# Up projection of a float32 encoder layer: both sequences together at each k tile instead of one after the other

## The reference

```python
up = _dwconv3(_rmsnorm(x, norm2) @ w_up, conv_w, conv_b)
gate, val = up[..., :D_FF], up[..., D_FF:]
x = x + (jax.nn.silu(gate) * val) @ w_down
```

## Time and profile before

| What | Value |
|---|---|
| median of 3 runs | 1347.67 us |
| span of the profiled execution, first to last instruction | 1343.5 us |
| TensorE busy | 1277.8 us, 95% of the span |
| VectorE busy | 820.0 us, 61% |
| ScalarE busy | 443.2 us, 33% |
| mean granted TensorE clock | 0.984 of full speed |
| matmuls and weight loads | 5487 each |

### The profile page before, as it was taken

One profiled execution on the slowest core, in us unless ns is written; L12 is line 12 of the kernel. 1 busy time (PEld: TensorE's weight loads), 2 busy tenths in 40 slices (PEclk: granted clock), 3 DMA queues, 4 the chain that ended last, 5 costly groups with the idle time before them and its releaser, 6 DMA issues.

```text
span 1343.5 us, 15745 instructions
## 1 busy us (share of the span) xinstructions
PE 1277.8 (95%) x5487; PEld 980.3 (73%) x5487; DVE 820.0 (61%) x1234; ACT 443.2 (33%) x711; POOL 175.3 (13%) x139
## 2 busy tenths in 40 slices
PE   6899699999999999999999999999999999979996
PEld 4687455555488778888888888888888888767885
DVE  5547786786456666565656565656565656594564
ACT  4311464564412352222222222222223231363233
POOL 0137400000065301010101010000000000060000
PEclk9999799999999999999999999999999999989999
DMA  5420000010343221111111111111111111012432
GB/s 177 174 55 10 10 11 0 10 31 1 110 141 94 95 79 47 48 47 47 47 47 47 47 47 47 47 47 47 47 47 47 47 47 47 8 32 82 130 112 91
DMA packets 103258, 78.76 MB, mean 59 GB/s; under 512 B 4707, under 2 KB 97210, under 8 KB 102458
## 3 DMA queue, kind: packets, MB, share of 16 engines
q1 hardware_dynamic: 102928, 78.23, 18.5%
q10 hardware_dynamic: 298, 0.11, 0.0%
HBM read 69.94 MB, written 8.39 MB: 58 GB/s over the span
## 4 chain that ended last, share of the span: by engine, by line
PE 79%; DVE 8%; issue 1%; ACT 1%; DVEq 0%; ACTq 0%
PE ps L184 24%; PE ps L186 24%; PE ps L185 24%; PE ps L491 3%; PE ps L479 2%; DVE XL L1372 1%; DVE XT L1208 1%; DVE SF L1185 1%; DVE XT L1188 1%; DVE XT L1184 1%; DVE XT L1333 1%; DVE col L1201 0%; DVE WDHL L1194 0%; DVE TL L1422 0%; PE ps L378 0%
## 5 line engine op out<-in xcount | busy, mean ns | idle before, releaser
L184 PE MATMUL ps<-XH,WH 128*128 128x512 f32 x1096 | 441.8, 403 | 5.3 <-DVE SF L1100 3.7
L185 PE MATMUL ps<-XL,WH 128*128 128x512 f32 x1096 | 436.5, 398 | 0.0
L186 PE MATMUL ps<-XH,WL 128*128 128x512 f32 x1096 | 436.3, 398 | 0.0
L184 PEld LDWEIGHTS ps<-XH,WH 128*128 128x128 f32 x1096 | 207.9, 190 | 59.1 <-DVE WL L197 6.5
L185 PEld LDWEIGHTS ps<-XL,WH 128*128 128x128 f32 x1096 | 207.8, 190 | 51.1 <-issue 1.9
L186 PEld LDWEIGHTS ps<-XH,WL 128*128 128x128 f32 x1096 | 207.7, 189 | 50.6
L1303 DVE TENSOR_TENSOR SF<-ps,R 128x512 f32<-128x512 f32 x88 | 60.6, 690 | 178.9 <-PE ps L186 173.4
L943 ACT ACTIVATE SF<-SF,col 128x512 f32<-128x512 f32 x88 | 71.8, 817 | 268.0 <-DVE SF L1303 268.0
L197 DVE TENSOR_TENSOR WL<-WR,WH 128x1024 fp32r<-128x1024 f32 (+2 forms) x93 | 119.8, 1293 | 61.9 <-ACT WH L192 61.9
L1333 DVE TENSOR_TENSOR XT<-XT,ps 128x512 f32<-128x512 f32 x176 | 116.7, 685 | 63.0 <-PE ps L186 63.0
L192 ACT ACTIVATE WH<-WR 128x1024 fp32r<-128x1024 f32 (+2 forms) x93 | 93.1, 1002 | 187.7 <-PE ps L186 179.0
(11 more groups left out here) (153 smaller groups left out, 1361.7 us busy)
## 6 DMA issues: line engine op xcount, KB each, us to landing
WR<-in_w_up SPq DMA_DIRECT2D x44, 512.0 KB, 3.8
SF<-in_w_down SPq DMA_DIRECT2D x11, 1024.0 KB, 4.9
WR<-in_w_out SPq DMA_DIRECT2D x16, 512.0 KB, 3.8
WR<-in_w_ple_gate SPq DMA_DIRECT2D x16, 512.0 KB, 3.9
WR<-in_w_in SPq DMA_DIRECT2D x8, 512.0 KB, 3.9
xt_scratch<-XT SPq DMA_DIRECT2D x2, 2048.0 KB, 13.0
XT<-xt_scratch SPq DMA_DIRECT2D x4, 1024.0 KB, 7.8
out<-TL SPq DMA_DIRECT2D x8, 512.0 KB, 2.7
```

What stands on the lines that cost most here:

```text
L184: pe.matmul(out, wh, xh, start=first, stop=False)
L185: pe.matmul(out, wh, xl, start=False, stop=False)
L186: return pe.matmul(out, wl, xh, start=False, stop=last)
```

## The change

A new function `up_both(i, c)` replaces `up(i, c)` for all up tiles but the first two of pair 0, which is 42 of 44. At each k tile it issues, for sequence 0 and then 1, high weights times the high and the low activation half; then low weights times the high half for both sequences. Both banks fill at the same time. The number of matmuls, their shapes and operands are the same. It waits once, for the banks of both sequences, ahead of its first matmul. `up_ready` is signalled by the last two matmuls.

```diff
+            def up_both(i, c):
+
+                n = T_UP + c
+                pe.wait_ge(w_lo, i * 4 + (n + 1))
+                if c >= 2:
+                    pe.wait_ge(u_ready, i * 8 + 2 * (c - 1))
+                else:
+                    pe.wait_ge(u_ready, i * 8 + (2 * c - 2))
+                for k in range(KT):
+                    wh, wl = WH[:, slot(n), k, :], WL[:, slot(n), k, :]
+                    for s in range(NSEQ):
+                        b = ps[2 * (c % 2) + s][:, :]
+                        pe.matmul(b, wh, XH[:, s, k, :], start=k == 0, stop=False)
+                        pe.matmul(b, wh, XL[:, s, k, :], start=False, stop=False)
+                    for s in range(NSEQ):
+                        b = ps[2 * (c % 2) + s][:, :]
+                        ins = pe.matmul(b, wl, XH[:, s, k, :], start=False, stop=k == KT - 1)
+                        if k == KT - 1:
+                            ins.then_inc(up_ready, 1)
+
...
-            up(0, 2)
-            up(0, 3)
+            up_both(0, 2)
+            up_both(0, 3)
             with pe.Fori(0, NPAIR // 2) as j:
                 for i in (j * 2 + 1, j * 2 + 2):
-                    up(i, 0)
-                    up(i, 1)
+                    up_both(i, 0)
+                    up_both(i, 1)
                     down(i - 1, 0)
                     down(i - 1, 1)
-                    up(i, 2)
-                    up(i, 3)
+                    up_both(i, 2)
+                    up_both(i, 3)
```

## The result

The changed kernel takes 1354.39 us (median of 5 runs, 1352.93 to 1355.83), the kernel before 1347.66 us (median of 5, 1344.03 to 1348.14). The ratio is 1.0049 with a 95% interval of 1.0036 to 1.0061: slower by 4.9 to 8.2 us.

A forecast was written before the change was run, and what follows sets the result against it. TensorE was taken as the bound, busy for all 512.80 us of the loop window, with no cover left at down tile 6. 1347.67 + 4.5 (ten holes) + 0.45 (last down) = 1352.6 us, range 1349.0 to 1357.0.

The forecast's parts named there:

- Step between matmuls: Up tiles: each matmul keeps its own weight load and the 234 ns step, bank switches costing 0.
- The faster rival: Up tiles: matmuls that repeat their weights come cheaper, 14.1 us saved less 4.95, giving 1338.5 us; chance 6%.
- the slower ones: Up tiles: alternating banks adds 12.1 us, 1364.7 us, chance 5%; or the clock falls to 1.2 GHz, adding 383 us, 1%.
- Delay of the adds: VectorE behind up tile 1: both `scaled` come behind the tile's end, so down's adds begin 0.45 us late.
- The pattern of pair 0: Pair 0 runs two `scaled` back to back, next work 4.27 us behind the first: lower bound of delay, 0.39 us.
- the loop's own ScalarE latency: In the loop ScalarE's middle tap begins 0.81 us behind the start of `scaled`: upper bound of delay, 0.49 us.
- One hole per pair, at down tile 6: TensorE stands 0.45 us at down tile 6, waiting for the third add, in 10 pairs: 4.5 us.
- Tile 4 with its 0.2 us of cover: Down tile 4: the delayed first add is done at 795.87, its weight load starts at 796.10, so just hidden.
- The last down: Outside the loop, TensorE's 4.61 us wait for the split of the gated result ends 0.45 us later.
- The sum: Whole kernel: +4.5 and +0.45 make +4.95 us on the median 1347.67, giving 1352.6 us.
- time outside the first and last instruction: Whole kernel: the median of the runs was taken as 4.2 us above the profiled span of 1343.5 us.
- The clock at the end: Behind the last down's wait: stretches at 1.2 GHz shift with the program, given ±1.6 us with mean 0.

The follow-up runs named there:

- the third add first: Changed kernel, and separately the kernel before, with VectorE's add of down tile 2 moved ahead of the next low-weight split: 1347.48 us and 1347.43 us.
- the first experiment: Changed kernel with up tile 1 inside the loop back to one sequence after the other, tiles 0, 2 and 3 still interleaved: 1348.82 us, ratio 1.0001.
- the second: Changed kernel with only up tile 1 of pairs 1 to 10 interleaved, all other up tiles in the old order: 1353.36 us, ratio 1.0036.

## Why the prediction was right, point by point

**Step between matmuls.** I took 234 ns for both orders. Right: up tile 1 takes 11.24 us in both, a pair with all up tiles interleaved takes 66.79 us where it takes 66.79 in the old order (both with the third add first), and the equality of loads and matmuls held. The faster rival (held weights pay) and the slower ones (banks, the clock) are out. The Trainium skill says in "TensorE: Matmul & The Clock Gate", section "Step-by-step: what each phase is for", that weights typically stay put over many matmuls, so that one load can serve them; this program issued a load for each, and nothing was gained. The same page of the Trainium skill tells, under "A second HAM failure mode: psum-queue depth-cycling", of a kernel whose clock swung while it cycled through banks; that did not come here, where the granted clock in the loop was 1.00 with the banks alternated.

**Delay of the adds.** Taken 0.45 us, bounds 0.39 and 0.49; measured 0.47. The pattern of pair 0 gave the lower bound, the loop's own ScalarE latency the upper one, and the truth lay nearer to the loop's.

**One hole per pair, at down tile 6.** Right in place and count, 0.48 us against 0.45; the wait of the weight load is 0.65 to 0.70 us where I wrote about 0.6. Tile 4 with its 0.2 us of cover did not wait.

**The last down.** +0.45 predicted, 5.08 - 4.61 = +0.47 measured. That it does not come from up tile 1 is shown by the first experiment, where it stays, and by the second, where it is gone. That of the other tiles it is up tile 3, the one directly ahead, was not tested by itself.

**The sum.** +4.95 predicted; 10 x 0.48 + 0.47 = 5.3 us by the trace. The runs give +6.7 us, interval 4.9 to 8.2, so the trace's 5.3 lies in it. The forecast of 1352.6 us is 1.8 us below the measured 1354.39, and 1.4 us of this is more than the mechanism explains. A part may be the median of before, which rests on five runs: the larger groups of runs beside the experiments give 1348.50 and 1348.22 us for the same kernel, 5.9 and 6.2 us below 1354.39.

One figure of the base was wrong: "time outside the first and last instruction" was taken as 4.2 us. In the profile after, the profiled execution itself took 1354.68 us with a span of 1352.8, so 1.9 us lie outside, and the runs of the kernel before that give both show about 2 (1344.03 and 1342.0). The profiled execution of before was then probably a short one of about 1345.4 us. The sum was made as a difference to the median, and so the mistake fell out of it. That also explains why the two spans differ by 9.3 us and the medians by 6.7.

**The clock at the end.** ±1.6 us. The profiled execution after had 0.74 of full clock in the 20 us in which the last down ends and the gate stage begins, and before had 0.83:

```profile
1208.90:1228.90 20.00, 13.96 (x53) 11.03 (x52) 11.65 (x17) 6.86 (x12) 7.75 (x6) 0.74 0.14 40
```

```profile
1200.20:1220.20 20.00, 13.98 (x56) 11.08 (x55) 12.07 (x18) 7.49 (x13) 7.75 (x6) 0.83 0.14 41
```

From the start behind the last down's wait to the end of the span it is 167.15 us after (1352.85 - 1185.70) and 166.49 before (1343.50 - 1177.01), 0.66 us more, well inside the ±1.6. Over all nine profiled executions (before, after, seven experiments) the three with 0.74 in this stretch take 167.15 to 167.46 us and the six with 0.83 take 166.27 to 166.61. So the clock here is worth about 1 us from one execution to the next. It is not tied to the longer wait: the kernel with only tile 1 interleaved has 0.74 with the wait of before. Whether it shifts the median of the changed kernel one profile can't say. What I had left out is the same effect ahead of the loop; the last section has it.

## What to carry to other kernels

Look first at where a consumer waits with no cover left, and count an edit by what it does to the last signal in front of that place; TensorE's order within the 11 us of an up tile changed nothing else here. A wait of 0.2 us in a list of waits can mean that the cover is just used up: here it cost 0.05 us per pair, and every delay beyond it counted in full, once in each pair: adds 0.47 us late cost 0.48 us, and adds 0.71 us late cost 0.72. A cure can be to move one instruction that is needed now ahead of one whose result is needed some 25 us later.

## What the runs showed of the hardware

The first down of the loop starts between 523.51 and 527.54 us in the nine profiled executions. The four up tiles ahead of it, the first that the change touches, account for none of this: they take 45.08 us in all nine, in the old order and the new. In the kernel before and in the changed one they begin at

```profile
478.43 0.50 PE L184 MATMUL ps<-XH,WH 128*128 128x512 f32 x1 [1.64 <-DVE WL L197]
```

```profile
481.88 0.50 PE L600 MATMUL ps<-XH,WH 128*128 128x512 f32 x1 [1.63 <-DVE WL L197]
```

and up to there all nine kernels do the same. The mean granted clock up to 523.5 us is 0.98 in the kernel before and 0.97 in the changed one:

```profile
0.00:523.50 523.50, 479.32 (x2027) 334.92 (x2028) 339.93 (x556) 213.48 (x390) 113.43 (x103) 0.98 0.21 66
```

```profile
0.00:523.50 523.50, 479.85 (x2013) 335.00 (x2014) 339.30 (x555) 212.05 (x389) 113.32 (x103) 0.97 0.20 65
```

The difference lies in the first 366 us; from there to 523.5 us the granted clock is 1.00 in all nine. Up to 366 us it is 0.97 in the two executions whose down starts first (523.51 and 524.08), 0.96 in two others (525.08 and 526.96) and 0.95 in the remaining five (525.32 to 527.54). The start goes with the clock, but not strictly. I read the clock's low stretches in the stages with idle time as the main reason for these 4 us, for the spread of the kernel before (1344.03 to 1348.14 us) and for intervals of 0.1% or more; it was not tested by a run of its own. The loop itself is exact: its period repeats within 0.05 us from pair to pair (66.83 to 66.86 us before, 67.31 to 67.34 after), and a difference of 0.05 us between kernels can be read from it that no median shows.

That held weights save nothing, with four matmuls in sequence on one set and a load for each, was the other finding. Whether the loads would be saved if they were not issued was not tried.
